# A two-model network on one core: expert numbers on GpSimd, rows restored by ScalarE, and 18 more gathered rows summed by TensorE

## The chip, the cores and the metric

The kernel runs on one core of a Trainium2 chip. The time is the device time of one execution in microseconds (us). Executions of the same kernel are compared by their median; lower is better. The core has five engines that work at the same time, each with its own queue of instructions: TensorE (PE, with its weight loads as PEld), VectorE (DVE), ScalarE (ACT), GpSimd (POOL) and SyncE (SP, which only issues DMAs). They meet at semaphores. Sixteen DMA engines move data between HBM and the core's memory.

## The reference, cut to what matters

Two networks of depth 2 run one after the other over 256 tokens of width 1024 in fp32. The change lies in the first one's expert layer (`_peer`) and in the work that is run beside it.

```python
def _peer(h, wq, sub_k1, sub_k2, u_tab, v_tab):
    q = (h @ wq).reshape(Bb, S, PEER_HEADS, 2, PEER_HALF)
    s1 = jnp.einsum('bshd,hnd->bshn', q[..., 0, :], sub_k1).astype(jnp.float32)
    s2 = jnp.einsum('bshd,hnd->bshn', q[..., 1, :], sub_k2).astype(jnp.float32)
    v1, i1 = lax.top_k(s1, PEER_TOPK)
    v2, i2 = lax.top_k(s2, PEER_TOPK)
    cand_s = (v1[..., :, None] + v2[..., None, :]).reshape(Bb, S, PEER_HEADS, PEER_TOPK * PEER_TOPK)
    cand_e = (i1[..., :, None] * PEER_N_KEYS + i2[..., None, :]).reshape(Bb, S, PEER_HEADS, PEER_TOPK * PEER_TOPK)
    top_s, pos = lax.top_k(cand_s, PEER_TOPK)
    experts = jnp.take_along_axis(cand_e, pos, axis=-1)
    g = jax.nn.softmax(top_s, axis=-1)
    ...
        u = jnp.take(u_tab, eb, axis=0)
        act = jax.nn.gelu(jnp.einsum('tkd,td->tk', u, hb), approximate=False)
        vv = jnp.take(v_tab, eb, axis=0)
        return jnp.einsum('tk,tkd->td', gb * act, vv)
```

Each token picks 8 heads x 16 = 128 experts. For each it needs a row of `u_tab` (a dot with the token's h) and a row of `v_tab` (added with its weight). The expert's number is i1 * 128 + i2 of the chosen pair. Around that stand attention, a short convolution, modulation by a condition (`ada`), and layer norms. The second network (`second_block`) has a pass over 256 context tokens, which does not depend on the first network, and a pass over the latent tokens, which follows it.

## The kernel before, in words

**Tiles and stages.** 256 tokens are two tiles t of 128 (one token on each partition). For each layer l and tile t there are two gather stages: `stage(l, t, 0, plan)` (dots with rows of `peer_u`) and `stage(l, t, 1, plan)` (sums of rows of `peer_v`). A stage has 32 rounds of 4 picks. For each pick GpSimd issues one indirect DMA (L1322), which fetches 128 rows of 4 KB, one for each token, into one of NS = 9 slots (six in RING, three at the end of WORK; the trace names them RING and WORK). VectorE makes the dot (`dots`, L2055) from the slot and the token's h, which lies in `hrows` (HB, two banks of PSUM), and writes the result to ACTS. In a sums stage (`sums`, L2073) it adds rows in turn to ACC and to HB. A slot is free for the gather nine later when it has been read. GpSimd has nothing else to do: its queue holds gathers in order, each behind a wait for its slot, the first of a group of 32 also behind `routed`.

**What is run beside them.** VectorE's order is written out by hand. `plan` maps a round to steps, which are Python generators: after round k's dots or sums the next piece of each named generator is issued. `c0` is the context pass of layer 0, `c1` the keys and values of the context for layer 1, `a` is `tile1(1, t)`, all of layer 1 for tile t up to its routing (with `closing` for the last norm of a tile), `choices` the routing groups of layer 0. Routing (`route`) treats 2 of 8 heads at a time: 4 groups a tile, 16 in all, 5 steps each: the top 16 of each half's 128 scores, the 256 sums of pairs, their top 16, and then the numbering (L2020 to L2030): with the place of the pick in the 16 x 16 table split into two places BF, VectorE compares each with iota, multiplies by the index TIF and adds up, once for each half. Of layer 0's groups one runs before the first dots stage and seven beside it, one or two steps a round; layer 1's groups run beside the two sums stages after.

**TensorE and SyncE.** TensorE works through a stream of weight chunks of 1 MB; SyncE loads them in the same order, three chunks ahead. TensorE's order is: layer 1's modulation, the context pass, `tile1(1, 0)`, `tile1(1, 1)`, the rest of the context pass, `c1`, then the latent pass. It also takes part in two sums stages: of the picks in `BY_PE`, 24 in stage (0, 1) and 36 in stage (1, 0), it multiplies the slot by a diagonal matrix of the weights (DIAG, made by ScalarE, L1623) into two banks (L882), and VectorE folds these into ACC (L2100).

**ScalarE** copies banks out of PSUM, in an order of its own. In the first dots stage it runs `ada("b1", [0], FIRST)` to its end before it comes to `gelu(0, 0)`, which closes the stage.

**The end of a sums stage** (VectorE): HB += ACC (L2102), HB *= gate (L2104), X = ALPHA * X + HB (L2106), moments of X (L2116 to L2124). At the start of the next dots stage the next tile's h is copied from HN to HB (L2081). `scaled_rows` (L2138, L2141) and `standard` (L2148, the y that TensorE waits for in `tile1`) are the first steps of `a`.

## Time and profile before

| | us |
|---|---|
| median of 3 runs | 2729.15 (2726.39 to 2731.91) |
| the profiled execution | 2727.62 |
| its span, first to last instruction | 2725.6 |
| first dots stage, layer 0 tile 0 | 216.0 to 496.4 |
| sums of layer 0 tile 0 | 496.4 to 725.2 |
| dots, sums of layer 0 tile 1 | 731.8 to 941.6, to 1161.0 |
| dots, sums of layer 1 tile 0 | 1168.7 to 1379.6, to 1585.0 |
| dots, sums of layer 1 tile 1 | 1592.5 to 1823.5, to 2025.1 |
| latent pass | 2025.1 to 2725.6 |

Busy time over the span: TensorE 1869.9 us (69%), VectorE 1862.3 us (68%), GpSimd 1074.6 us (39%), ScalarE 405.3 us (15%). DMA moves 850.48 MB, 538.17 MB of it gathers issued by GpSimd and 310.76 MB mostly weights issued by SyncE.

How to read the rows: a window row gives the busy time of each engine in a stretch, with the number of instructions, then TensorE's granted clock as a share of full speed, the busy share of the DMA engines (it can pass 1 a little) and what they moved. A timeline row gives start, duration, engine, source line, operation, what it writes and reads, shape, count, and in brackets the engine's idle time before it with what ended it. A group row gives busy time, the mean in ns of one, and idle time before.

### The profile page before, as it was taken

How to read it: one execution, taken by the hardware profiler on the slowest of the kernel's cores; microseconds unless marked ns; L12 is line 12 of the kernel's file. 1: busy time of each engine (PE TensorE's matmuls, PEld its weight loads, DVE VectorE, ACT ScalarE, POOL GpSimd, SP SyncE). 2: the span in 40 equal slices, each digit the busy share in tenths (PEclk: the TensorE clock that was granted, in tenths of full speed). 3: DMA queues.
4: the chain of work that ended last, by engine and by line, in shares of the span. 5: the costliest groups of instructions: out<-in, count | busy, mean ns of one | idle time of the engine just before them, and what ended most of it. 6: DMA issues, size and time to landing. Idle time of an engine off the chain costs nothing.

```text
span 2725.6 us, 24342 instructions
## 1 busy us (share of the span) xinstructions
PE 1869.9 (69%) x8469; PEld 1349.1 (49%) x8469; DVE 1862.3 (68%) x3405; ACT 405.3 (15%) x911; POOL 1074.6 (39%) x1059
## 2 busy tenths in 40 slices
PE   7988444385554373744635789774409999999998
PEld 5777111164443161233333277632307887578873
DVE  2758998879878879988888986778985342253001
ACT  1321001123103011012111010000104100141000
POOL 2004435567556555755565764556740000000000
PEclk9999556595776675967767999887659999999999
DMA  9629999999899999999999999999963694333443
GB/s 341 236 78 361 399 399 400 397 367 396 310 395 404 399 401 400 383 340 403 404 397 367 381 367 400 400 409 384 346 267 110 222 302 143 135 110 105 150 148 123
DMA packets 347386, 850.48 MB, mean 312 GB/s; under 512 B 23832, under 2 KB 126592, under 8 KB 347136
## 3 DMA queue, kind: packets, MB, share of 16 engines
q0 software_dynamic: 148672, 538.17, 51.1%
q1 hardware_dynamic: 198592, 310.76, 32.3%
q8 instruction: 68, 1.11, 0.2%
q14 instruction: 54, 0.44, 0.0%
HBM read 847.79 MB, written 1.05 MB: 311 GB/s over the span
## 4 chain that ended last, share of the span: by engine, by line
PE 29%; DMA 28%; DVE 21%; issue 14%; POOL 5%; ACT 1%; SPq 1%; DVEq 0%; POOLq 0%; ACTq 0%
DMA RING<-in_peer_u,EX 12%; DMA RING<-in_peer_v,EX 11%; PE bank L1174 10%; PE bank L1193 6%; POOL RING L1322 4%; DVE ACC L2055 3%; DMA WORK<-in_peer_u,EX 3%; PE bank L453 3%; DVE hrows L2073 2%; PE bank L1098 2%; POOL WORK L1322 2%; DMA WORK<-in_peer_v,EX 1%; PE bank L917 1%; PE bank L462 1%; PE bank L441 1%
## 5 line engine op out<-in xcount | busy, mean ns | idle before, releaser
L2055 DVE SCALAR_TENSOR_TENSOR ACC<-RING,hrows 128x1024 bf16<-128x1024 f32 x343 | 408.5, 1219 | 103.1 <-DMA RING<-in_peer_u,EX 96.2
L1322 POOL DMA_INDIRECT RING<-in_peer_u,EX x343 | 325.0, 948 | 350.2 <-DVE ACC L2055 244.1
L1322 POOL DMA_INDIRECT RING<-in_peer_v,EX x341 | 377.2, 1106 | 198.9 <-DVE hrows L2073 77.6
L1174 PE MATMUL bank<-HT,W 128*128 128x256 f32 x1280 | 276.6, 379 | 0.0
L1174 PEld LDWEIGHTS bank<-HT,W 128*128 128x128 f32 x1280 | 243.0, 190 | 33.0
L490 PE MATMUL bank<-W,CACT 128*32 128x512 f32 x544 | 115.2, 946 | 199.7 <-DMA W<-in_w_ada 115.4
L1193 PE MATMUL bank<-W,WORK 128*128 128x512 f32 x528 | 228.9, 596 | 18.6 <-DVE WORK L2763 16.2
L2055 DVE SCALAR_TENSOR_TENSOR ACC<-WORK,hrows 128x1024 bf16<-128x1024 f32 x169 | 202.1, 1218 | 47.5 <-DMA WORK<-in_peer_u,EX 46.5
L1322 POOL DMA_INDIRECT WORK<-in_peer_v,EX x171 | 194.3, 1137 | 99.1 <-DVE hrows L2073 41.7
L1322 POOL DMA_INDIRECT WORK<-in_peer_u,EX x169 | 160.9, 952 | 157.5 <-DVE ACC L2055 136.0
L2073 DVE SCALAR_TENSOR_TENSOR ACC<-RING,ACTS,ACC 128x1024 f32<-128x1024 f32 x148 | 189.9, 1283 | 35.3 <-DMA RING<-in_peer_v,EX 34.2
L2073 DVE SCALAR_TENSOR_TENSOR hrows<-RING,ACTS,hrows 128x1024 f32<-128x1024 f32 x147 | 189.1, 1286 | 29.9 <-DMA RING<-in_peer_v,EX 28.9
L441 PE MATMUL bank<-consts,XN 128*128 128x128 f32 x152 | 32.2, 387 | 239.5 <-DVE XN L2148 117.0
L1156 PE MATMUL bank<-HT,W 128*128 128x256 f32 x704 | 160.6, 390 | 20.7 <-DVE WORK L2763 14.0
L1193 PEld LDWEIGHTS bank<-W,WORK 128*128 128x128 f32 x528 | 100.7, 191 | 145.5 <-issue 142.4
L2769 DVE TENSOR_TENSOR WORK<-WORK,bank 128x256 f32<-128x256 f32 x44 | 18.5, 421 | 223.9 <-ACT WORK L1769 223.9
L1156 PEld LDWEIGHTS bank<-HT,W 128*128 128x128 f32 x704 | 136.6, 196 | 44.4 <-issue 22.0
L744 PE MATMUL bank<-HT,W 128*128 128x128 f32 x832 | 119.9, 313 | 51.6 <-DMA W<-in_peer_wq 27.8
L441 PEld LDWEIGHTS bank<-consts,XN 128*128 128x128 f32 x152 | 26.9, 204 | 242.0 <-DVE XN L2148 117.8
L490 PEld LDWEIGHTS bank<-W,CACT 128*32 128x32 f32 x544 | 14.7, 134 | 263.6 <-DMA W<-in_w_ada 99.7
L744 PEld LDWEIGHTS bank<-HT,W 128*128 128x128 f32 x832 | 117.0, 228 | 55.4 <-DMA W<-in_peer_wq 27.3
L1357 ACT ACTIVATE WORK<-bank 128x512 f32<-128x512 f32 (+5 forms) x167 | 87.4, 542 | 378.9 <-PE bank L744 124.5
(438 smaller groups left out, 3017.6 us busy)
## 6 DMA issues: line engine op xcount, KB each, us to landing
W<-in_ada_w SPq DMA_DIRECT2D x36, 1024.0 KB, 16.3
W<-in_w_gate SPq DMA_DIRECT2D x33, 1024.0 KB, 8.3
W<-in_w_up SPq DMA_DIRECT2D x33, 1024.0 KB, 5.5
W<-in_w_down SPq DMA_DIRECT2D x33, 1024.0 KB, 5.0
W<-in_w_in SPq DMA_DIRECT2D x32, 1024.0 KB, 16.4
W<-in_w_ada SPq DMA_DIRECT2D x32, 1024.0 KB, 16.9
W<-in_peer_wq SPq DMA_DIRECT2D x24, 1024.0 KB, 18.2
W<-in_w_o SPq DMA_DIRECT2D x10, 1024.0 KB, 15.9
```

Source lines behind the costliest of these rows:

```text
L441: mm = pe.transpose(b[0:rows, j * P:(j + 1) * P], a, ident)
L453: mm = pe.matmul(b[:, t * 256:t * 256 + cols], hT[:, k, t * P:(t + 1) * P], w[:, k, 0:cols], start=(k == 0), stop=(k == K - 1))
L490: mm = pe.matmul(b[32 * k:32 * k + 32, :], CACT[:, 4 * c + k, :], w[:, k, :], start=(c == 0), stop=(c == 1), skip_group_check=True)
L744: mm = pe.matmul(b[:, at:at + P], w[:, k, at:at + P], HT[:, 4 * c + k, T], start=first, stop=(c == 1 and k == 3), skip_group_check=True)
L1098: mm = pe.matmul(b[:, at_ * 256:(at_ + 1) * 256], HT[:, k, t * P:(t + 1) * P], w[:, k, :], start=(k == 0), stop=(k == DC - 1))
L1156: mm = pe.matmul(bs[u][:, e * S:(e + 1) * S], w[:, k, at_:at_ + P], HT[:, nk * part + k, :], start=(part == e == k == 0), stop=(part == n ...
L1174: mm = pe.matmul(bs[j][:, g * S:(g + 1) * S], w[:, k, j * P:(j + 1) * P], HT[:, k, :], start=(k == 0 and g == 0), stop=(k == DC - 1 and g ...
L1193: mm = pe.matmul(bs[2 * t + hf][:, :], GU[:, 2 * c + k, t * P:(t + 1) * P], w[:, k, hf * 512:(hf + 1) * 512], start=(c == 0 and k == 0), s ...
L1322: gp.indirect_dma_start(SLOT[g % NS], None, rows, bass.IndirectOffsetOnAxis(EX[:, t, k:k + 1], 0))\
L1357: free(name, A(out_, b[:, :] if src is None else src(b), ACT.Copy, scale=scale))
L2055: ve.scalar_tensor_tensor(out=JUNK[:, g % 2, :], in0=SLOT[g % NS], scalar=1.0, in1=HB[:, :], op0=ALU.mult, op1=ALU.mult, accum_out=ACTS[:, ...
L2073: ins = ve.scalar_tensor_tensor(out=acc, in0=SLOT[g % NS], scalar=ACTS[:, k:k + 1], in1=acc, op0=ALU.mult, op1=ALU.add)
```

## The change

It has three parts.

**Expert numbers.** Both halves' comparisons are done in one instruction over 1024 numbers into a larger EQ; the index of the first half is scaled by 128 and shifted by the layer's offset beforehand (TIF). For layer 0's seven groups beside the first dots stage VectorE stops after the comparison (`picked`), and GpSimd multiplies and adds in seven instructions, each behind the one before (`expert_numbers`), in its own queue between two gathers: `NUMBERED_AT` puts a group's numbering ahead of the gather that is nine behind the first pick of the second round after the comparison. VectorE waits for `routed` of the group before in the fourth step of each group, as TIF and EQ are used again. The other nine groups stay on VectorE in the wider form. ScalarE's `gelu(0, 0)` comes after three steps of `ada("b1", [0], FIRST)`, the rest after it.

**The seam.** At the end of a sums stage the total goes to ACC; ScalarE then copies HN to HB (`rows_again`), VectorE waits for that and writes the gated total to HN. Adding it to X and the moments are a step of their own (`into_rows`), the first of `a`, after round 0 of the next stage.

**The last sums stage.** TensorE also sums 18 picks of stage (1, 1), picks 36 to 70, every other one (`diagonal_rows(2)`), ahead of `c1` in its order. The result is folded in after round 19. The steps of `c1` and the first latent rows come later (22 instead of 14, 24 instead of 18), and some steps of `c0` in the stage before one or two rounds sooner.

Semaphores that can be shared are merged, and a few steps of the context pass are moved by one or two rounds. The diff, cut to its core:

```diff
-        BY_PE = {(0, 1): [78 + 2 * i for i in range(24)], (1, 0): [54 + 2 * i for i in range(36)]}
+        SHARED = [(0, 1), (1, 0), (1, 1)]
+        BY_PE = {(0, 1): [78 + 2 * i for i in range(24)], (1, 0): [54 + 2 * i for i in range(36)],
+                 (1, 1): [36 + 2 * i for i in range(18)]}
...
+        ROUTE_STEPS = 5
+        FIRST_STEPS = [1 + k % 2 for k in range(PICKS // 4)]
+        LATER_ROUNDS = [8 + (23 * i) // 20 for i in range(ROUTE_STEPS * GROUPS)]
+        def round_of_first(step):
+            return next(k for k in range(len(FIRST_STEPS)) if sum(FIRST_STEPS[:k + 1]) > step)
+        NUMBERED_AT = {}
+        for i_, (t_, g_) in enumerate([(0, g) for g in range(1, GROUPS)] + [(1, g) for g in range(GROUPS)]):
+            NUMBERED_AT[gather(0, 0, 0, 4 * (round_of_first(ROUTE_STEPS * i_ + 3) + 2)) + NS] = (0, t_, g_)
+        def groups_routed(l, t, g):
+            return (l * NT + t) * GROUPS + g
+        def expert_numbers(eng, do, settle, l, t, g):
+            do(eng.tensor_tensor(EQ, EQ, TIF.unsqueeze(2).to_broadcast([P, GSETS, TOPK, TOPK]), ALU.mult))
+            settle()
+            eq = EQ.rearrange("p (h e) k a -> p h e k a", e=2)
+            part = eq[:, :, 0, :, :]
+            do(eng.tensor_tensor(part, part, eq[:, :, 1, :, :], ALU.add))
+            width = TOPK
+            while width > 1:
+                width //= 2
+                settle()
+                do(eng.tensor_tensor(part[:, :, :, 0:width], part[:, :, :, 0:width], part[:, :, :, width:2 * width], ALU.add))
+            settle()
+            do(eng.tensor_copy(EX[:, t, g * GP:(g + 1) * GP].rearrange("p (h k) -> p h k", h=GHEADS), part[:, :, :, 0]),
+               mark("routed", "all"))
         def place(n):
...
+            def diagonal_rows(u):
+                ls, ts = SHARED[u]
+                picks = BY_PE[ls, ts]
+                bs = [open_bank(("sum", ("b1", u), hf), "V") for hf in range(2)]
+                pe.wait_ge(mark("diag", "b1"), u + 1)
+                for i, k in enumerate(picks):
+                    g = gather(ls, ts, 1, k)
+                    pe.wait_ge(rows_in[g % NS], 16 * (g // NS + 1))
+                    for hf in range(2):
+                        mm = pe.matmul(bs[hf][:, :], DIAG[u][:, i, :], SLOT[g % NS][:, hf * 512:(hf + 1) * 512],
+                                       start=(i == 0), stop=(i == len(picks) - 1))
+                        if hf == 0 and i == len(picks) - 1:
+                            mm.then_inc(filled, 1)
+                    mm.then_inc(slots_passed, 1)
+                pe.matmul(bs[1][0:1, 0:1], ident[0:1, 0:1], ident[0:1, 1:2], start=False, stop=True, skip_group_check=True).then_inc(filled, 1)
...
             last_rows.append(nrows[0])
+            diagonal_rows(2)
...
+                            if g in NUMBERED_AT:
+                                lg, tg, group = NUMBERED_AT[g]
+                                gp.wait_ge(mark("picked", "all"), groups_routed(lg, tg, group))
+                                expert_numbers(gp, do, settle, lg, tg, group)
                             if table == 0 and k % GP == 0:
-                                gp.wait_ge(mark("routed", f"b{l}"), t * GROUPS + k // GP + 1)
+                                gp.wait_ge(mark("routed", "all"), groups_routed(l, t, k // GP) + 1)
                             if g >= NS:
...
+            def rows_again(i):
+                act.wait_ge(mark("totalled", "all"), i)
+                do(A(HB[:, :], HN[:, :], ACT.Copy), mark("restored", "all"))
...
             weigh(0, 0)
-            all_of(ada("b1", [0], FIRST))
+            first = ada("b1", [0], FIRST)
+            for _ in range(3):
+                next(first)
             gelu(0, 0)
+            all_of(first)
             spread_rows()
...
             next(c0)
+            rows_again(1)
             root1("b0", 0, 7)
...
                 if t:
+                    rows_again(2)
                     root1("b0", t, 7 + t)
...
             spread_rows()
+            rows_again(3)
...
-                bp = BP.rearrange("p h k -> p (h k)")
-                do(ve.tensor_scalar(BQ[:, 0, :], bp, 4, None, ALU.logical_shift_right))
-                do(ve.tensor_scalar(BQ[:, 1, :], bp, TOPK - 1, None, ALU.bitwise_and))
-                settle()
-                do(ve.tensor_copy(BF, BQ))
+                n = groups_routed(l, t, g)
+                if n:
+                    ve.wait_ge(mark("routed", "all"), n)
+                tif = TIF.rearrange("p (h e) k -> p h e k", e=2)
+                ti = TI.rearrange("p (h e) k -> p h e k", e=2)
+                do(ve.tensor_scalar(tif[:, :, 0, :], ti[:, :, 0, :], float(KEYS), float(l * EXPERTS), ALU.mult, ALU.add))
+                do(ve.tensor_copy(tif[:, :, 1, :], ti[:, :, 1, :]))
+                do(ve.tensor_scalar(BQ[:, :, 0, :], BP, 4, None, ALU.logical_shift_right))
+                do(ve.tensor_scalar(BQ[:, :, 1, :], BP, TOPK - 1, None, ALU.bitwise_and))
+                settle()
+                do(ve.tensor_copy(BF.rearrange("p (h e) k -> p h e k", e=2), BQ))
                 do(ve.tensor_tensor(GW[:, t, picks].rearrange("p (h k) -> p h k", h=GHEADS), BV,
                                     BV[:, :, 0:1].to_broadcast([P, GHEADS, TOPK]), ALU.subtract),
                    v_step if g < GROUPS - 1 else mark("tx", p))
                 settle()
+                where = [P, GSETS, TOPK, TOPK]
+                by_gpsimd = 0 < n < NT * GROUPS
+                do(ve.tensor_tensor(EQ, BF.unsqueeze(3).to_broadcast(where),
+                                    const("iota").unsqueeze(1).unsqueeze(1).to_broadcast(where), ALU.is_equal),
+                   mark("picked", "all") if by_gpsimd else v_step)
                 yield
-                tif = TIF.rearrange("p (h e) k -> p h e k", e=2)
-                eq = EQ.rearrange("p (h k a) -> p h k a", h=GHEADS, k=TOPK)
-                eqn = EQ.rearrange("p (n a) -> p n a", a=TOPK)
-                for e in range(2):
-                    do(ve.tensor_tensor(eqn, BF[:, e, :].unsqueeze(2).to_broadcast([P, GP, TOPK]),
-                                        const("iota").unsqueeze(1).to_broadcast([P, GP, TOPK]), ALU.is_equal))
-                    settle()
-                    do(ve.tensor_tensor(eq, eq, tif[:, :, e, :].unsqueeze(2).to_broadcast(full), ALU.mult))
-                    settle()
-                    do(ve.tensor_reduce(EF[:, e, :], eqn, AX.X, ALU.add))
-                    settle()
-                do(ve.scalar_tensor_tensor(out=EF[:, 0, :], in0=EF[:, 0, :], scalar=float(KEYS), in1=EF[:, 1, :],
-                                           op0=ALU.mult, op1=ALU.add))
-                settle()
-                do(ve.tensor_scalar(EX[:, t, picks], EF[:, 0, :], float(l * EXPERTS), None, ALU.add), mark("routed", p))
+                if not by_gpsimd:
+                    settle()
+                    do(ve.tensor_tensor(EQ, EQ, TIF.unsqueeze(2).to_broadcast(where), ALU.mult))
+                    settle()
+                    do(ve.tensor_reduce(EF, EQ, AX.X, ALU.add))
+                    settle()
+                    ef = EF.rearrange("p (h e) k -> p h e k", e=2)
+                    do(ve.tensor_tensor(EX[:, t, picks].rearrange("p (h k) -> p h k", h=GHEADS), ef[:, :, 0, :], ef[:, :, 1, :], ALU.add),
+                       mark("routed", "all"))
                 yield
...
+            def fold(u):
+                for hf in range(2):
+                    b = wait_full(ve, ("sum", ("b1", u), hf))
+                    c = slice(hf * 512, (hf + 1) * 512)
+                    free(("sum", ("b1", u), hf), ve.tensor_tensor(ACC[:, c], ACC[:, c], b[:, :], ALU.add))
+                settle()
+            def last_fold(k):
+                ve.wait_ge(slots_free, vector_done(gather(1, 1, 1, PER * (k + 1))))
+                fold(2)
+                yield
             def stage(l, t, table, plan):
                 p = f"b{l}"
-                if table == 0 and (l or t):
-                    do(ve.tensor_copy(HB[:, :], HN[:, :]))
-                    settle()
...
-                if (l, t) in SHARED:
-                    q = ("b1", SHARED.index((l, t)))
-                    for hf in range(2):
-                        b = wait_full(ve, ("sum", q, hf))
-                        c = slice(hf * 512, (hf + 1) * 512)
-                        free(("sum", q, hf), ve.tensor_tensor(ACC[:, c], ACC[:, c], b[:, :], ALU.add))
-                    settle()
-                do(ve.tensor_tensor(HB[:, :], HB[:, :], ACC[:, :], ALU.add))
-                settle()
-                do(ve.tensor_tensor(HB[:, :], HB[:, :], GA[:, GATES[p, 0][1], :], ALU.mult))
-                settle()
-                do(ve.scalar_tensor_tensor(out=X[:, t, :], in0=X[:, t, :], scalar=ALPHA, in1=HB[:, :],
+                if (l, t) in SHARED[:2]:
+                    fold(SHARED.index((l, t)))
+                last = l == LAYERS - 1 and t == NT - 1
+                do(ve.tensor_tensor(ACC[:, :], HB[:, :], ACC[:, :], ALU.add), v_step if last else mark("totalled", "all"))
+                settle()
+                if not last:
+                    ve.wait_ge(mark("restored", "all"), n[mark("totalled", "all").name])
+                do(ve.tensor_tensor(HN[:, :], ACC[:, :], GA[:, GATES[p, 0][1], :], ALU.mult))
+                settle()
+            def into_rows(l, t):
+                p = f"b{l}"
+                do(ve.scalar_tensor_tensor(out=X[:, t, :], in0=X[:, t, :], scalar=ALPHA, in1=HN[:, :],
                                            op0=ALU.mult, op1=ALU.add))
                 settle()
                 moments(p, t)
...
+                into_rows(l - 1, t)
+                yield
                 scaled_rows(f"b{l - 1}", t)
...
+                if p == "c0":
+                    ve.wait_ge(mark("routed", "all"), groups_routed(1, 0, 0))
                 if who == "c":
...
-                    if not kv_only:
+                    if kv_only:
+                        yield
+                    else:
                         yield from gate_rows(p, (1, 2))
...
             def closing(l, t):
+                into_rows(l, t)
+                yield
                 scaled_rows(f"b{l}", t)
                 yield
...
-            stage(0, 0, 1, {k: [c0] for k in (0, 3, 5, 10, 16, 20, 21, 25, 31)})
+            stage(0, 0, 1, {k: [c0] for k in (0, 5, 6, 11, 16, 20, 21, 25, 31)})
             for t in range(NT):
                 a = tile1(1, t)
-                stage(t, 1 - t, 0, {k: [a] for k in (0, 1, 4, 11, 12, 14, 16, 17, 19, 23, 28)})
-                plan = {**{k: [a] for k in (0, 1)}, **{8 + (23 * i) // 20: [a] for i in range(5 * GROUPS)}}
+                stage(t, 1 - t, 0, {k: [a] for k in (0, 1, 2, 4, 11, 12, 14, 16, 17, 19, 23, 28)})
+                plan = {k: [a] for k in (0, 1, *LATER_ROUNDS)}
                 if t:
                     plan[15] = plan.get(15, []) + [c0]
                 stage(t, 1 - t, 1, plan)
                 finish(a)
             a = closing(1, 0)
-            stage(1, 1, 0, {0: [a], **{k: [c0] for k in (4, 5, 9, 10, 13, 14, 18, 19, 22, 23, 26)}})
-            stage(1, 1, 1, {6: [c0], 8: [c0], 10: [c1], 14: [c1], 18: [first_rows()]})
+            stage(1, 1, 0, {**{k: [a] for k in (0, 1)}, **{k: [c0] for k in (4, 5, 9, 10, 13, 14, 17, 18, 21, 22, 24)}})
+            stage(1, 1, 1, {6: [c0], 8: [c0], 10: [c1], 11: [c1], 19: [last_fold(19)], 22: [c1], 24: [first_rows()]})
             finish(c0, c1, closing(1, 1))
             for p, l in (("l0", 0), ("l1", 1)):
```

## Rows read from the trace of the kernel before

**Rows 1.** Page, 40 slices of the span: busy tenths of the DMA engines

```profile
DMA  9629999999899999999999999999963694333443
```

**Rows 2.** Windows: the gather half, then D00, S00, S01, D11 and S11

```profile
216.00:2025.10 1809.10, 1012.79 (x4295) 684.70 (x4293) 1543.83 (x2738) 234.65 (x522) 1053.86 (x1021) 0.74 1.00 386
216.00:496.40 280.40, 151.67 (x665) 79.30 (x664) 255.12 (x697) 31.15 (x60) 125.37 (x134) 0.62 1.03 396
496.40:725.20 228.80, 140.90 (x650) 112.36 (x648) 192.66 (x201) 46.56 (x116) 153.22 (x128) 0.72 1.01 384
...
941.60:1161.00 219.40, 120.55 (x538) 74.39 (x538) 193.46 (x364) 26.03 (x63) 138.08 (x125) 0.74 1.02 395
...
1592.50:1823.50 231.00, 194.05 (x780) 151.38 (x779) 165.94 (x275) 11.73 (x18) 120.36 (x128) 0.92 1.02 397
1823.50:2025.10 201.60, 76.31 (x246) 46.76 (x244) 175.37 (x165) 15.82 (x33) 134.65 (x119) 0.69 0.96 370
```

**Rows 3.** DMA queues from 1625 to 1700 us: packets, MB, share of 16 engines

```profile
q0 software_dynamic: 5328, 19.40, 66.0%
q1 hardware_dynamic: 5327, 10.58, 37.1%
```

**Rows 4.** Timeline of VectorE in S11, two sums back to back

```profile
1885.79 1.28 DVE L2073 SCALAR_TENSOR_TENSOR ACC<-RING,ACTS,ACC 128x1024 f32<-128x1024 f32 x1
1886.99 1.28 DVE L2073 SCALAR_TENSOR_TENSOR hrows<-RING,ACTS,hrows 128x1024 f32<-128x1024 f32 x1
```

**Rows 5.** Timeline of VectorE from S00's last sum to the second dot of D01

```profile
725.16 1.23 DVE L2102 TENSOR_TENSOR hrows<-hrows,ACC 128x1024 f32<-128x1024 f32 x1
...
730.58 1.22 DVE L2081 COPY hrows<-HN 128x1024 f32<-128x1024 f32 x1
731.84 1.22 DVE L2055 SCALAR_TENSOR_TENSOR ACC<-RING,hrows 128x1024 bf16<-128x1024 f32 x1
...
732.98 1.22 DVE L2055 SCALAR_TENSOR_TENSOR ACC<-RING,hrows 128x1024 bf16<-128x1024 f32 x1
```

**Rows 6.** Timeline of GpSimd in S11, two gather issues

```profile
1964.37 0.93 POOL L1322 DMA_INDIRECT RING<-in_peer_v,EX  x1 [0.30 <-issue]
1965.61 1.99 POOL L1322 DMA_INDIRECT RING<-in_peer_v,EX  x1 [0.31 <-DVE hrows L2073]
```

**Rows 7.** Timeline of VectorE, first and last of the eight of a group's numbering

```profile
206.53 0.69 DVE L2020 TENSOR_TENSOR WORK<-WORK,consts 128x512 f32<-128x512 f32 x1
...
211.10 0.18 DVE L2030 TENSOR_SCALAR EX<-WORK 128x32 uint32<-128x32 f32 x1
```

**Rows 8.** Window: D00 while groups are routed

```profile
216.00:440.20 224.20, 127.55 (x557) 67.27 (x559) 215.54 (x628) 24.29 (x47) 95.39 (x102) 0.64 1.03 395
```

**Rows 9.** Windows: a stretch of S00, and S00's last sum to D01's y

```profile
550.00:575.00 25.00, 23.45 (x109) 20.06 (x108) 21.11 (x18) 3.77 (x8) 19.82 (x18) 0.99 0.93 336
714.90:747.70 32.80, 4.47 (x37) 4.18 (x35) 29.95 (x51) 7.31 (x12) 8.50 (x9) 0.60 0.66 241
```

**Rows 10.** Timeline of ScalarE: the third step's copy, and the table load of gelu

```profile
461.84 0.17 ACT L1357 ACTIVATE CR<-bank 128x4 f32<-128x4 f32 x1 [1.17 <-PE bank L499]
...
493.29 1.28 ACT L1638 ACT_TABLE_LOAD   x1
```

**Rows 11.** Window: S10 with routing beside it

```profile
1465.00:1530.00 65.00, 36.17 (x69) 13.15 (x70) 62.67 (x151) 5.36 (x19) 43.67 (x40) 0.84 0.94 351
```

**Rows 12.** Timeline of ScalarE: one pass over 128x1024

```profile
2033.72 1.06 ACT L1375 ACTIVATE XN<-X 128x1024 f32<-128x1024 f32 x1 [2.88 <-DVE X L2141]
```

**Rows 13.** S11 from round 8 on: the window, and GpSimd's larger group there

```profile
1884.60:2025.10 140.50, 29.00 (x112) 24.03 (x112) 132.15 (x125) 10.00 (x23) 99.16 (x89) 0.59 0.94 356
...
L1322 POOL DMA_INDIRECT RING<-in_peer_v,EX x60 | 67.1, 1119 | 25.9 <-issue 15.5 <-DVE hrows L2073 10.3
```

**Rows 14.** Timeline of TensorE in S10, its first rows and a later one

```profile
1479.97 8.30 PE L882 MATMUL bank<-RING,WORK 128*128 128x512 f32 x12 [20.95 <-DMA RING<-in_peer_v,EX]
...
1491.57 1.98 PE L882 MATMUL bank<-RING,WORK 128*128 128x512 f32 x4 [1.59 <-DMA RING<-in_peer_v,EX]
```

86 lines of the change are left out of this document (37 added, 49 removed).

## The prediction, made before the changed kernel was run

> **What bounds the kernel now.** I read the page first: the DMA engines are busy 90% or more in nearly all slices from the fourth to the twenty-ninth (204 to 1976 us), and a third to a half near the end [rows 1]. So there are two halves. Up to 2025 us rows of the expert tables are gathered; from there on TensorE is busy nearly all the time, and nothing in the change touches that. Then I cut the first half at the eight gather stages. I call them D00, S00, D01, S01, D10, S10, D11, S11 (D dots, S sums; layer, tile). Each gathers 128 times a row of 4 KB for 128 tokens, 0.524 MB. In all eight the DMA share is 0.96 to 1.03, at 370 to 397 GB/s; the rows show five of them, the lowest and the highest among them [rows 2]. The forecast rests on that: VectorE is busy 72 to 91% of the stages, but beside a queue that is as full.
>
> How full is full? In a stretch of D11 in which VectorE mostly waits, the gathers get 19.40 MB in 75 us (259 GB/s, a row in 2.03 us) and the weights 10.58 MB (141 GB/s), 400 GB/s together [rows 3]. Without weights a row costs 0.524/0.400 = 1.31 us. VectorE needs 1.19 us for a sum issued back to back and 1.14 us for a dot, GpSimd 0.94 us for an issue and 0.30 us between two [rows 4 to 6]. These rates lie close together, so time freed on VectorE is worth only what DMA then moves more. The first half moves 386 GB/s over 1809 us, 698 MB [rows 2]; at 400 GB/s that is 1745 us. The 64 us between are the most that could be found here, and they are spread thin.
>
> **Part 1, expert numbers.** Sixteen routing groups. The numbering of one is eight VectorE instructions from 206.53 to 211.28 us, 4.75 us [rows 7]. The new form handles all 1024 numbers at once. An instruction over 128x1024 takes 1.22 to 1.23 us and 0.04 to the next [rows 5], so compare, multiply and reduce cost 3 x 1.26, the last add 0.2, one more small scaling 0.1: 4.1 us, a gain of 0.65 us for each of nine groups. Of the seven groups routed beside D00, VectorE keeps the compare and the scaling, 1.36 us instead of 4.75: 3.4 us each, 23.8 us together. Until 440 us VectorE is busy 215.5 of 224.2 us there, so it paces the dots [rows 8]. With 23.8 us less D00 would last 256.6 us; but beside unbounded weights 128 rows need 128 x 2.03 = 260 us. D00 becomes about 20 us shorter.
>
> That is not 20 us of the kernel. D00's DMA share is 1.03 with 111 MB [rows 2]. If it ends 20 us sooner, 8 MB of weights have not come, and S00 wants them, for layer 1's modulation and for the context block. D00 and S00 together move 199 MB in 509.2 us; at 400 GB/s it is 497.5, so at most 11.7 us can be had. What keeps S00 below that (336 GB/s while TensorE is busy 23.5 of 25 us with the context block's projections [rows 9]) isn't touched. I take 5 us, bounds 0 and 12.
>
> What GpSimd's seven arithmetic instructions for a group cost, no row shows. The nearest rows are its own issues: 7 x (0.94 + 0.30) = 8.7 us [rows 6]. From below, VectorE's 1.23 us for 1024 elements [rows 5], scaled to the 2048 of all seven, is 2.5 us; from above, an issue of 1.99 us gives 7 x 2.3 = 16 us [rows 6]. I take 8.7 us. Queued behind it are the gathers: with nine slots up to 9 x 2.03 = 18 us of rows are on their way, so 8.7 us without an issue starves nothing. VectorE waits for it only in the fourth step of the next group; between lie at least eight dots (9.1 us) and three steps of some 3 us, about 18 us. The page GPSIMD Engine Reference of the Trainium skill (section 3.1) speaks against the move: a two-input elementwise pass takes 2.6 cycles an element at 1.2 GHz there, about twice VectorE's time. By it the 2048 elements are an estimated 4.5 us and what seven starts cost; no row of this kernel shows that.
>
> On ScalarE, `gelu` is moved ahead of the second half of layer 1's first modulation. Now ScalarE reaches it at 493.3 us, 1.8 us before the dots end; the three steps that then stand ahead of it end at 462 us [rows 10]. Without that, it would be late by what D00 gains. Its price: two banks stay uncopied until D00 ends, and the rows for the context block's second step (round 5, no longer 3) come later. A wait there leaves the bandwidth to the weights; I cost it at nothing, and it is why the 12 us are not reached. If that cover is gone, it is the 5 us.
>
> The layer 1 groups lie beside S01 and S10, 4 x 0.65 = 2.6 us each, partly in stretches where VectorE is busy 63 of 65 us and DMA moves 351 GB/s [rows 11]: 1.5 us in S01 (395 GB/s) and 2.5 us in S10, bounds 0 and 5 for both.
>
> **Part 2, the seam from sums to the next dots (three times).** Now 725.16 to 731.84 us, 6.7 us [rows 5]. Afterwards: the add (1.26), then a copy into hrows by ScalarE that VectorE waits for (nearest row 1.06 us over 128x1024 [rows 12], with the hand-over 1.3), then the multiply (1.26), 3.8 us. The rest, 2.9 us, is done after four dots. VectorE drops its own copy of 1.22 us and gains a wait of 1.3, so its line is not shorter. Slots come free 2.9 us sooner, but TensorE gets the tile's y after twelve dots instead of eight, 4.6 us later. The window from the last sums to y moves 241 GB/s [rows 9], so there is room; yet what is gained ahead of the moved step is given back in it. I take 0 for D01 and D10 and 1 us for D11, where TensorE awaits no y. Bounds: 3 x 2.9 = 8.7 us gained, 3 us lost.
>
> **Part 3, S11.** From round 8 (1884.6 us) to the end 96 rows and a few weights, 356 GB/s x 140.5 us = 50 MB, pass with VectorE busy 132.2 us [rows 13]. TensorE takes 18 rows, 18 x 1.19 = 21.4 us, and the fold adds 2 x 0.69 (the nearest row is 128x512 [rows 7]): VectorE 112 us. DMA needs 50/0.400 = 125 us. So the bound passes to DMA, or to GpSimd, whose issue takes 1.12 us here [rows 13] and 0.30 between: 1.42 us a row, 136 us if it stayed so slow. I take 129.5 us, a gain of 11, bounds 5 and 15. TensorE's price for a row is 1.98 us, one every 2.62 us; the first three after idleness take 8.3 us, in which slots are held [rows 14]. The diagonals are made by ScalarE behind `gelu`, long before round 9. The context keys (round 22, not 14) and the latent rows (24, not 18) come later; TensorE has 28 rows x 1.31 = 37 us for what follows, some 20 us of transposes and projections, so nothing sticks out past the last sum. If it did, it would cost up to 13 us. The context block's steps in D11 that come one or two rounds sooner move no bytes. The chain after S11 (add, multiply, residual, norm) has the same length.
>
> **Sum.** 5 + 1.5 + 2.5 + 1 + 11 = 21 us. The profiled run took 2727.6 us for a span of 2725.6, 1.5 us under the median of 2729.15; from the median it gives **2708 us**.
>
> **Rivals.**
> 1. D00's gain carries through, 20 us and not 5: the deferred weights find room. 2729 - 36 = 2693 us. For it: S00 moves 384 GB/s. Against: D00's share of 1.03 [rows 2].
> 2. Gathers are bound by GpSimd's issue once VectorE is eased, D00 gives nothing, S11 6 us and the routing 4: 2719 us. For it: 1.42 us a row in S11 [rows 13].
> 3. Slower: the numbering takes GpSimd T a group. In the 3.3 rounds of a group it must also issue 13.3 rows, 13.3 x 1.24 = 16.5 us. From T = 18 us on, seven periods of 16.5 + T use up the 16 us that the other parts bring; at T = 20 us the routed part of D00 is 7 x 36.5 = 255 us, not 224, and the kernel takes 2729 + 31 - 16 = 2744 us. The place is the fourth step of each group, where VectorE would wait on `routed`. Against: 20 us is above the bound of 16.
> 4. TensorE's rows ease little, as S11 waits for DMA already: 3 us there, 10 elsewhere, 2716 us. Against: 356 GB/s [rows 13].
>
> The page DMA: Bandwidth & Descriptors of the Trainium skill (section Queues, rings and completion order) says that a DMA engine takes turns between its rings packet by packet. The trace agrees in that the split stays near 259 to 141 GB/s. By that rule weights put off by D00 come at a fixed share beside the gathers, which speaks against rival 1.
>
> **Chances.** Forecast 0.58, rival 1 0.12, rival 2 0.12, rival 4 0.10, rival 3 0.08. About 0.2% (5.5 us) is what a measurement of this kernel can tell from no change. Faster by more, under 2723.7 us, are the forecast and rivals 1, 2 and 4 less their tails: 0.84; within 0.2%, those tails and mild cases of rival 3: 0.10; slower 0.06. The range goes from 2691 us (rival 1) to 2723 us (rival 2 with S11 near its lower bound); rival 3 is left out.
>
> **What would show it.** D00 at 256 to 264 us with the DMA share still near 1.0, and S00 longer by 10 to 18 us; GpSimd's arithmetic at 6 to 12 us a group; seams of 3.8 us, with D01 and D10 as long as before, the 2.9 us inside; S11 at 188 to 192 us, VectorE idle for rows, over 385 GB/s after round 8; from the last sum on 700 us as now. It would be wrong if VectorE waited for GpSimd in D00, if S00 stayed at 229 us, or if DMA stayed under 360 GB/s in S11 after round 8.

## The result and the profile after

The changed kernel takes 2711.4 us, the median of 4 runs (2706.26 to 2713.43), beside 2727.77 us for the kernel before on the same chip: a ratio of 0.995, with a 95% interval from 0.9936 to 0.9964. That is 14 us less by the ratio, 16 by the medians; 21 were forecast. Measured again on another chip it came to 2710.67 beside 2723.41 us, 0.9959 (0.9943 to 0.9975), 11 to 13 us. The profiled execution took 2706.26 us for a span of 2704.3, the fastest of its four.

Windows of the changed kernel, in the columns of [rows 2]: the gather half, then D00, S00, S01, S10 with its seam, D11, S11 and the part of S11 from round 8 on.

```profile
212.30:2006.80 1794.50, 1044.89 (x4371) 694.21 (x4369) 1491.94 (x2653) 243.39 (x544) 1084.78 (x1070) 0.75 1.01 389
212.30:485.40 273.10, 134.20 (x595) 68.62 (x593) 233.54 (x654) 29.71 (x56) 164.20 (x183) 0.64 1.03 397
485.40:721.60 236.20, 154.77 (x720) 120.42 (x720) 194.70 (x203) 49.67 (x122) 150.03 (x128) 0.74 1.02 388
933.50:1156.40 222.90, 119.93 (x546) 73.36 (x546) 194.71 (x356) 27.37 (x65) 140.10 (x129) 0.75 1.02 397
1369.70:1581.40 211.70, 132.70 (x529) 83.08 (x530) 183.82 (x352) 32.00 (x78) 140.84 (x130) 0.83 1.01 384
1581.40:1817.00 235.60, 205.77 (x801) 156.50 (x800) 168.49 (x280) 11.13 (x17) 120.92 (x128) 0.93 1.02 396
1817.00:2006.80 189.80, 98.96 (x286) 53.16 (x284) 155.12 (x149) 21.26 (x51) 128.44 (x119) 0.78 1.00 381
1874.70:2006.80 132.10, 66.63 (x186) 37.05 (x186) 111.68 (x109) 10.08 (x23) 98.69 (x89) 0.76 0.98 373
```

VectorE works 22 us less in D00 and 20 us less in S11 than in [rows 2], and the whole half is only some 15 us shorter: the DMA share was 1.00 already and is 1.01 now. The table gives each stage from its first row to the next stage's first row, so a seam counts with the stage ahead of it. "First" is the first dot, "tail" what follows the last sum. The kernels under the second line are those of the experiments, one profiled execution each.

| us | first | D00 | S00 | D01 | S01 | D10 | S10 | D11 | S11 | tail |
|---|---|---|---|---|---|---|---|---|---|---|
| before | 216.0 | 280.4 | 235.5 | 209.8 | 227.1 | 210.9 | 212.9 | 231.0 | 201.6 | 700.5 |
| changed | 212.3 | 273.1 | 236.2 | 211.9 | 222.9 | 213.4 | 211.7 | 235.6 | 189.8 | 697.4 |
| changed, again | 215.1 | 271.7 | 238.8 | 211.4 | 223.1 | 213.2 | 208.5 | 235.6 | 189.1 | 701.2 |
| third part undone | 214.1 | 271.2 | 242.3 | 211.9 | 222.7 | 213.5 | 211.9 | 235.3 | 196.7 | 698.2 |
| numbers on VectorE | 213.2 | 278.9 | 235.5 | 212.4 | 222.6 | 213.0 | 208.4 | 235.4 | 190.8 | 701.7 |
| gelu behind one step | 211.8 | 266.9 | 244.8 | 212.1 | 222.6 | 212.8 | 213.0 | 236.0 | 191.4 | 701.8 |
| restore first | 216.0 | 269.6 | 241.7 | 211.9 | 222.8 | 213.1 | 206.2 | 236.8 | 188.5 | 701.8 |
| old seam | 213.8 | 270.4 | 240.4 | 208.8 | 225.6 | 211.1 | 208.9 | 235.5 | 188.2 | 697.6 |
| 26 rows | 213.6 | 270.9 | 240.1 | 211.8 | 222.8 | 213.7 | 212.0 | 236.3 | 190.5 | 701.2 |
| slow numbers | 213.5 | 295.7 | 228.3 | 211.5 | 222.6 | 213.4 | 210.3 | 235.4 | 188.9 | 700.7 |
| sums in PSUM | 214.2 | 272.2 | 239.1 | 211.5 | 223.0 | 212.8 | 208.8 | 236.7 | 190.3 | 701.4 |
| third part alone | 215.7 | 290.6 | 233.1 | 209.8 | 225.7 | 211.6 | 206.5 | 235.0 | 190.5 | 700.6 |
| half rows | 215.8 | 241.7 | 233.5 | 212.4 | 222.6 | 213.1 | 213.0 | 236.5 | 187.8 | 701.3 |
| three together | 213.5 | 269.6 | 237.7 | 212.2 | 222.6 | 213.6 | 207.3 | 236.6 | 189.7 | 700.6 |

Where the code of a stage is the same, the first dot lies between 211.8 and 216.0 us, S10 between 208.4 and 213.0 and the tail between 697.4 and 701.8: these scatter by 4 to 5 us from one execution to the next. So do the first two stages: D00 and S00 together take 507.4 to 513.5 us in the seven traces of kernels that leave them as changed, and of the kernel before there is one trace, with 515.8. D01, S01, D10 and D11 repeat within 2 us. The changed kernel's profiled execution had luck at both ends (most of 3.7 us, and 3.1), which is why its span is 21 us under that of before and its median only 16.

Two things in it were not foreseen. First, the end of D00: VectorE's last dot, its wait for gelu, and the first sum; then ScalarE, with what it waited for.

```profile
476.40 1.22 DVE L2118 SCALAR_TENSOR_TENSOR ACC<-RING,hrows 128x1024 bf16<-128x1024 f32 x1 [0.81 <-DMA RING<-in_peer_u,EX]
...
485.11 0.29 DVE L2166 TENSOR_TENSOR ACTS<-ACTS,GW 128x128 f32<-128x128 f32 x1 [6.54 <-ACT ACTS L1690]
485.44 1.29 DVE L2134 TENSOR_SCALAR hrows<-RING,ACTS 128x1024 f32<-128x1024 f32 x1
```

```profile
481.44 0.60 ACT L1400 ACTIVATE ROWT<-bank 128x512 f32<-128x512 f32 x1 [14.37 <-PE bank L522]
483.21 0.17 ACT L1400 ACTIVATE CR<-bank 128x4 f32<-128x4 f32 x1 [1.17 <-PE bank L531]
483.40 1.28 ACT L1690 ACT_TABLE_LOAD   x1
```

The three steps that stand ahead of gelu ended at 462 us before [rows 10] and at 483.4 us now. They hang on TensorE, and TensorE on weights, which come later: up to 462 us SyncE's queue has moved 35.4 MB since D00 began, where it had moved 38.4 before, and the gathers 63.4 MB instead of 58.8. Second, the third seam:

```profile
1571.92 1.23 DVE L2172 TENSOR_TENSOR ACC<-hrows,ACC 128x1024 f32<-128x1024 f32 x1
1580.14 1.23 DVE L2176 TENSOR_TENSOR HN<-ACC,GA 128x1024 f32<-128x1024 f32 x1 [7.00 <-ACT hrows L1678]
1581.40 1.22 DVE L2118 SCALAR_TENSOR_TENSOR ACC<-RING,hrows 128x1024 bf16<-128x1024 f32 x1
```

```profile
1578.53 0.60 ACT L1400 ACTIVATE ROWS<-bank 128x512 f32<-128x512 f32 x1 [0.32 <-PE bank L466]
1579.02 1.02 ACT L1678 ACTIVATE hrows<-HN 128x1024 f32<-128x1024 f32 x1
```

VectorE waits 1.2 us for the restore at the first seam, 1.5 at the second and 7.0 at the third, where ScalarE's order puts four copies of norm rows ahead of it, and TensorE makes those only once it has finished its 36 rows of S10.

### The profile page after: what moved, and what is told of

It is laid out like the page before. It is cut to its first block, busy times and chain, and to the rows that moved or that the text cites. A ratio compares the mean times of both kernels' runs of the same rounds, so it can differ in the third digit from the quotient of the medians.

```text
span 2704.3 us, 24477 instructions
## 1 busy us (share of the span) xinstructions
PE 1895.4 (70%) x8543; PEld 1353.6 (50%) x8543; DVE 1809.6 (67%) x3317; ACT 413.6 (15%) x932; POOL 1105.8 (41%) x1108
## 3 DMA queue, kind: packets, MB, share of 16 engines
q8 instruction: 68, 1.11, 0.2%
## 4 chain that ended last, share of the span: by engine, by line
PE 34%; DMA 31%; DVE 15%; issue 11%; POOL 5%; ACT 2%; SPq 1%; DVEq 0%; POOLq 0%; ACTq 0%
DMA RING<-in_peer_u,EX 11%; PE bank L1210 10%; DMA RING<-in_peer_v,EX 9%; PE bank L1229 6%; DMA W<-in_ada_w 3%; POOL RING L1379 3%; PE bank L485 3%; DVE ACC L2118 3%; DMA WORK<-in_peer_u,EX 2%; DMA WORK<-in_peer_v,EX 2%; PE bank L494 2%; PE bank L1134 2%; POOL WORK L1379 2%; DVE hrows L2136 2%; PE bank L473 2%
## 5 line engine op out<-in xcount | busy, mean ns | idle before, releaser
L1379 POOL DMA_INDIRECT RING<-in_peer_v,EX x341 | 371.0, 1088 | 197.8 <-issue 72.3
L2136 DVE SCALAR_TENSOR_TENSOR ACC<-RING,ACTS,ACC 128x1024 f32<-128x1024 f32 x142 | 182.1, 1282 | 39.7 <-DMA RING<-in_peer_v,EX 39.1
L2136 DVE SCALAR_TENSOR_TENSOR hrows<-RING,ACTS,hrows 128x1024 f32<-128x1024 f32 x141 | 181.4, 1286 | 34.5 <-DMA RING<-in_peer_v,EX 33.8
L791 PE MATMUL bank<-RING,WORK 128*128 128x512 f32 x212 | 110.0, 647 | 95.8 <-DMA RING<-in_peer_v,EX 95.8
```

The lines of the kernel that those rows point to most:

```text
L791: mm = pe.matmul(bs[hf][:, :], DIAG[u][:, i, :], SLOT[g % NS][:, hf * 512:(hf + 1) * 512], start=(i == 0), stop=(i == len(picks) - 1))
L1379: gp.indirect_dma_start(SLOT[g % NS], None, rows, bass.IndirectOffsetOnAxis(EX[:, t, k:k + 1], 0))\
L2136: ins = ve.scalar_tensor_tensor(out=acc, in0=SLOT[g % NS], scalar=ACTS[:, k:k + 1], in1=acc, op0=ALU.mult, op1=ALU.add)
```

## The experiments

"Ratio" is always the kernel's time to that of the kernel before on the same chip, with the 95% interval. 0.001 is 2.7 us.

**The changed kernel again.** No edit.

> The changed kernel once more, so that single parts can be compared with it. 2711 us, within 3. Theory: the 6.5 us for which VectorE waits for gelu at the end of the first dots stage and the 7.0 us for which it waits for ScalarE's restore at the third seam come again, since both stand behind work of TensorE in ScalarE's order. The 3.7 us by which the first dot came earlier (212.3 instead of 216.0 us) and the 3.1 us of the latent pass are 0.65 us and 0 by the change and otherwise scatter: first dot near 214, latent pass near 700. Rival: they are the change's, and both come again to 0.5 us.

Measured: 2710.67 us, ratio 0.9959 (0.9943 to 0.9975). First dot at 215.1, tail 701.2: both were scatter. The two waits come again, somewhat shorter, 4.74 and 5.98 us.

**The third part undone.**

```diff
-        SHARED = [(0, 1), (1, 0), (1, 1)]
+        SHARED = [(0, 1), (1, 0)]
...
-            diagonal_rows(2)
...
-            diagonals(2)
...
-            stage(1, 1, 1, {6: [c0], 8: [c0], 10: [c1], 11: [c1], 19: [last_fold(19)], 22: [c1], 24: [first_rows()]})
+            stage(1, 1, 1, {6: [c0], 8: [c0], 10: [c1, c1], 14: [c1], 18: [first_rows()]})
```

> The third part undone: VectorE sums all 128 rows of the last sums stage, no diagonals for it, its steps in rounds 6, 8, 10, 14 and 18 as before; the first two parts stay. Theory (what TensorE takes is worth 11 us): the stage goes back to 201 us from 189.8, the kernel to 2722 us. Rival: part of the 11.8 us that the stage lost are weights that the dots stage before has taken (28.7 MB instead of 26.3 there, 6.9 instead of 9.3 in the sums): 2.4 MB are 6 us, then the stage takes only 196 us and the kernel 2717. Rival 4 of the prediction: 2714 us.

Measured: 2720.38 us, ratio 0.9993 (0.9979 to 1.0006), so 9 to 10 us more than the changed kernel, while S11 takes 196.7 us, as the rival said. Both hold in part: the time is the theory's, the stage the rival's. In the profiled executions the rest of the distance lies in S00 and S10, the stages that scatter; that it is nothing but scatter isn't shown. Without a single row on TensorE S11 is already 4.9 us shorter than in the kernel before. D11 has taken 2.3 MB of its weights and is 4.3 us longer, which fits, though no run tried the weights by themselves. The hardware queue in D11, before and with the third part undone:

```profile
q1 hardware_dynamic: 12727, 26.38, 29.9%
```

```profile
q1 hardware_dynamic: 13315, 28.65, 31.9%
```

So the third part itself is worth 7 us in the two last stages (432.0 us together here, 424.7 in the repeated run), nearly all of what lies between those and the 432.6 us of the kernel before.

**Numbers on VectorE**, in the wide form.

```diff
-            NUMBERED_AT[gather(0, 0, 0, 4 * (round_of_first(ROUTE_STEPS * i_ + 3) + 2)) + NS] = (0, t_, g_)
+            pass
...
-                by_gpsimd = 0 < n < NT * GROUPS
+                by_gpsimd = False
```

> The numbering of layer 0's seven groups stays on VectorE, in the wider form (4.1 us a group); all else as changed. VectorE has 7 x 2.7 = 19 us more in the first dots stage. Theory (the stage is bound by DMA after the change, and the first two stages share 198 MB): the dots take 278 us instead of 265, the wait of 6.5 us for gelu goes, and the first two stages together take 512 to 515 us instead of 509.3: 2714 to 2717 us. Rival A: VectorE's time carries through, 19 us less the wait of 6.5: 2724 us. Rival B: GpSimd's numbering brings nothing: 2711 us.

Measured: 2714.55 us, ratio 0.9969 (0.9959 to 0.998): 3 to 4 us more, with intervals that overlap. The dots of D00 take 277.6 us instead of 265.7, and the wait for gelu is gone, as the theory has it. 17 us more of VectorE's time in D00 cost 7.2 us there and 3.9 after S00 (514.4 us together instead of 510.5), little beyond the scatter of these two stages. Rival A, 2724 us, is excluded; that the numbering on GpSimd brings the kernel something (against rival B) is likely and not clear of noise.

**Gelu behind one step.**

```diff
-            for _ in range(3):
+            for _ in range(1):
                 next(first)
             gelu(0, 0)
```

> ScalarE issues gelu behind one step of layer 1's first modulation instead of three. Now the third step ends at 483.4 us, 5.1 us after VectorE has weights ready, since TensorE waits for weights until 479.4. The table load then lies beside the dots, and VectorE's wait of 6.5 us shrinks to under 0.5 us. Theory (the queue stays full in the wait: 400 GB/s from 475 to 490 us, so the weights have used it): the first sums stage gets back 4 to 6 of the 6.5 us, the kernel gains 0 to 2 us: 2710 us. Rival: the wait is on the path, all of it is gained: 2705 us.

Measured: 2712.68 us, ratio 0.996 (0.9948 to 0.9972), no gain. D00 and S00 of this kernel:

```profile
211.80:478.70 266.90, 131.31 (x588) 67.44 (x586) 233.47 (x655) 29.22 (x54) 164.43 (x183) 0.65 1.03 396
478.70:723.50 244.80, 159.76 (x736) 124.22 (x728) 195.44 (x203) 50.48 (x124) 146.22 (x128) 0.72 1.02 385
```

The wait is gone and D00 is 5 us shorter, S00 is 6 us longer, and the two take 511.7 us beside 510.5. So this wait of VectorE, during which DMA moved 399 GB/s (changed kernel, 475 to 490 us), cost nothing that could be measured.

**Restore ahead of the norm rows.**

```diff
-            spread_rows()
             rows_again(3)
+            spread_rows()
             root1("b1", 0, 9)
```

> At the third seam ScalarE restores h (its copy of HN into HB) before the four copies of norm rows, not behind them. Now VectorE waits 7.0 us there (the rows wait for TensorE, which makes them until 1578.5 us), at the other two seams 1.2 and 1.5 us. The wait shrinks to about 1.5 us. Theory (no weights are under way there, and the gathers move 155 to 219 GB/s from 1581 to 1591 us, so the queue is not full): the 5.5 us are gained, the seam takes 5 us instead of 10, and the dots stage after it stays at 234 us: the kernel 2705 to 2707 us beside 2711. Rival: the dots stage after it is bound by DMA and by TensorE's weights, which don't come sooner: no gain, 2711 us, and the dots stage gets 4 to 5 us longer, as at the other seams.

Measured: 2708.82 us, ratio 0.9942 (0.9926 to 0.9958). VectorE's wait falls to 1.16 us:

```profile
1577.62 1.22 DVE L2172 TENSOR_TENSOR ACC<-hrows,ACC 128x1024 f32<-128x1024 f32 x1
1580.01 1.23 DVE L2176 TENSOR_TENSOR HN<-ACC,GA 128x1024 f32<-128x1024 f32 x1 [1.16 <-ACT hrows L1678]
```

From the last sum to the next dot, with the fold, it is 5.0 us, not 10.8 and 9.8 as in the two runs of the changed kernel. D11 takes 1.2 us more, so 3.6 us should be left. The two kernels run beside it on the same chip, which both have the time of the changed one within the interval, took 2709.74 and 2709.93 us. What is left of the gain is 1 us by these medians and can't be told from none.

**The old seam**, with the rest as changed.

```diff
-                do(ve.tensor_tensor(ACC[:, :], HB[:, :], ACC[:, :], ALU.add), v_step if last else mark("totalled", "all"))
+                do(ve.tensor_tensor(HB[:, :], HB[:, :], ACC[:, :], ALU.add))
...
+                if table == 0 and (l or t):
+                    do(ve.tensor_copy(HB[:, :], HN[:, :]))
...
```

> The second part undone: at all three seams VectorE adds into HB, multiplies, adds to X, takes the moments and copies HN to HB itself before the next dots, 6.7 us; ScalarE's restore is gone, and so is the wait for it. The rest as changed. Theory of the prediction (0 + 0 + 1 us for the three seams): 2711 to 2713 us beside 2711; the first two seams get 2.5 to 2.9 us longer and the dots stages after them 2 to 2.5 us shorter; at the third the wait of 7.0 us goes, the seam takes 8 us instead of 9.8 to 11, and the kernel may even gain 1 to 2 us. Rival: the seam is worth its 2.9 us three times, 2718 us.

Measured: 2709.74 us, ratio 0.9948 (0.9933 to 0.9963). S01 with its seam is 2.5 us longer and D10 behind it 2.1 us shorter; D01 is 2.6 us shorter. The new seam is worth nothing that can be measured: at the first two the stage behind gives the gain back, and at the third the wait makes it longer than the old one (9.8 and 10.8 us with the fold, beside 8.0).

**26 rows instead of 18.**

```diff
-                 (1, 1): [36 + 2 * i for i in range(18)]}
+                 (1, 1): [36 + 2 * i for i in range(26)]}
...
-            stage(1, 1, 1, {..., 19: [last_fold(19)], 22: [c1], 24: [first_rows()]})
+            stage(1, 1, 1, {..., 23: [last_fold(23)], 25: [c1], 26: [first_rows()]})
```

> TensorE sums 26 rows of the last sums stage instead of 18 (picks 36 to 86, every other one); folded in after round 23 instead of 19, the next step of c1 in round 25 instead of 22, first latent rows 26 instead of 24. VectorE has 8 x 1.19 = 9.5 us less in the stage. Theory (18 rows have already handed the stage to DMA and to GpSimd's issue; 381 GB/s): the stage loses at most 2 us of 189.5, and what follows the fold lies closer to the end: 2709 to 2713 us. Rival: VectorE's time is still the bound; 18 rows brought 7.6 us, 0.42 us a row, so 8 rows bring 3.4 us: 2707 us.

Measured: 2709.93 us, ratio 0.9945 (0.9931 to 0.996); S11 190.5 us. VectorE is busy 145.5 instead of 155.1 us in it, and the stage is no shorter: 18 rows have used the effect up.

**Slow numbers.**

```diff
         def expert_numbers(eng, do, settle, l, t, g):
+            for _ in range(5):
+                do(eng.tensor_tensor(EQ, EQ, EQ, ALU.mult))
+                settle()
```

> GpSimd does five more passes over 128x1024 (EQ times EQ, which leaves its zeros and ones) ahead of each of the seven numberings: 6.04 + 5 x 2.4 = 18 us a group. It asks for the price in rival 3 of the prediction. Theory: a group's 13.3 rows take 27.6 us at the present pace, and GpSimd needs 16.5 + 18 = 34.6 us, so it becomes the bound: the first dots stage gets 7 x 7 = 49 us longer (320 us), weights come early in it, the first sums stage gets 20 to 28 us shorter (VectorE is busy 203 of its 238 us): the kernel 2731 to 2741 us. Rival: what 9 slots hold (18 us of rows) covers it and VectorE's wait on routed stays under 2 us a group: under 2715 us.

Measured: 2726.45 us, ratio 1.0014 (1.0003 to 1.0024), 16 us more than the changed kernel. The numbering of the changed kernel, then the five added passes and the last instruction of the slow one:

```profile
248.88 2.37 POOL L331 TENSOR_TENSOR WORK<-WORK 128x1024 f32<-128x1024 f32 x1
251.33 1.27 POOL L335 TENSOR_TENSOR WORK<-WORK 128x512 f32<-128x512 f32 x1
252.68 1.95 POOL L340 TENSOR_TENSOR WORK<-WORK 128x256 f32<-128x256 f32 x4
254.69 0.23 POOL L342 CAST EX<-WORK 128x32 uint32<-128x32 f32 x1
```

```profile
251.34 9.79 POOL L332 TENSOR_TENSOR WORK<-WORK 128x1024 f32<-128x1024 f32 x5
...
267.34 0.23 POOL L345 CAST EX<-WORK 128x32 uint32<-128x32 f32 x1
```

The numbering takes 6.0 us a group in the changed kernel and 16.2 us here. D00 is 24 us longer than in the repeated run, S00 10.4 shorter. VectorE never waits for `routed`; it waits for rows, 51 us instead of 32 in D00, that GpSimd issued late. GpSimd is busy 233 of D00's 296 us. Hence ten more microseconds a group take away all that the change has brought.

**Sums of S11 in PSUM only.**

```diff
-                    acc = ACC[:, :] if n % 2 else HB[:, :]
-                    ve.wait_ge(slots_free, n - 1)
+                    alone = (l, t) == (1, 1)
+                    acc = ACC[:, :] if n % 2 and not alone else HB[:, :]
+                    ve.wait_ge(slots_free, n if alone else n - 1)
...
```

> In the last sums stage VectorE adds every row to HB (in PSUM) and none to ACC (in SBUF); the fold copies TensorE's sum into ACC. Each sum then waits for the one before: 1.31 us apart instead of 1.19, 110 x 0.12 = 13 us more for VectorE. What is asked: why the stage's end moves only 374 to 384 GB/s. In the changed kernel GpSimd's issues that begin under a sum into HB take 0.936 us (34 of 34), those that begin under a sum into ACC, which reads two operands from SBUF, 1.35 us in the mean, three in four of them longer than 1 us. From 1870 to 2007 us GpSimd is in an issue or between two for 126 of 137 us. Theory (the stage's end is bound by GpSimd's issues, and they are held up by the sums into ACC): all issues of the stage take 0.94 us, 91 rows need 91 x 1.31 = 119 us by DMA instead of 126, the stage takes 181 to 185 us instead of 189, the kernel 2703 to 2707 us. Rival A: DMA is the bound anyway and the issues don't matter: 189 us, 2710. Rival B: VectorE's 13 us more decide: 195 us or more, 2716.

Measured: 2713.96 us, ratio 0.9961 (0.9948 to 0.9973); S11 190.3 us. GpSimd's issues into RING from round 8 on (busy time, mean ns, idle before), of the changed kernel and of this one:

```profile
L1379 POOL DMA_INDIRECT RING<-in_peer_v,EX x60 | 66.2, 1104 | 18.4 <-issue 16.5 <-DVE hrows L2136 1.5 <-PE bank L791 0.4
```

```profile
L1379 POOL DMA_INDIRECT RING<-in_peer_v,EX x60 | 57.3, 956 | 23.3 <-DVE hrows L2137 14.4 <-issue 7.6 <-PE bank L791 1.3
```

And a window of each after 1900 us, in which no weights come:

```profile
1901.00:1949.00 48.00, 29.25 (x81) 14.43 (x82) 35.16 (x30) 3.86 (x8) 37.20 (x36) 0.86 1.00 381
```

```profile
1904.00:1950.00 46.00, 28.55 (x83) 14.63 (x82) 34.34 (x28) 3.86 (x8) 34.57 (x37) 0.85 1.03 409
```

The first half of the theory is shown: the issues take 0.956 us instead of 1.104, and DMA goes from 381 to 409 GB/s. In that stretch of the changed kernel 36 issues and the 0.30 us between two fill the 48 us, so GpSimd was the bound there. The second half is not: the last row lands 183.5 us after the stage's start instead of 187.3 and 188.2, but VectorE, whose sums are now 1.39 us apart, needs another 6.8 us instead of 1.7. What the issues gave back, the slower sums took, so neither rival is right by itself: the bound went from GpSimd to VectorE.

**The third part alone** (numbers on VectorE, old seam, gelu last).

```diff
             first = ada("b1", [0], FIRST)
-            for _ in range(3):
-                next(first)
-            gelu(0, 0)
             all_of(first)
+            gelu(0, 0)
...
```

> The third part alone: as the kernel with the old seam, and in addition layer 0's numbering stays on VectorE (in the wider form, the one thing left of the first part) and gelu stands behind the whole first modulation again. Theory: the kernel without the third part was 9.7 us over the changed one, numbers on VectorE cost 3.9 us, the old seam nothing, so the third part is most of the change: 2713 to 2715 us beside 2710 for the changed kernel and 2722 for the kernel before. Rival: the parts hold each other up (the weights that the first part puts off meet the last stages), and the third alone brings less than 5 us: 2718 us.

Measured: 2719.21 us, ratio 0.9983 (0.9973 to 0.9993), 4 to 5 us under the kernel before: the rival's number, by another cause. D11 and S11 take 425.5 us, so the third part brings its 7 us here too. But VectorE waits 11.8 us for gelu at the end of D00:

```profile
504.05 1.28 ACT L1690 ACT_TABLE_LOAD   x1
```

The dots end at 493.0 us, 2 us sooner than before, and ScalarE comes to gelu 11 us later than before [rows 10], behind steps that wait for weights. D00 and S00 together take 523.7 us, beside 515.8 in the kernel before. The run with numbers on VectorE has the same numbering and 514.4 us. Of the 9.3 us between them, 3.0 are the old seam, which D01 gives back (209.8 us instead of 212.4); the rest goes with the place of gelu. So the new place is likely what lets the first part pay; the old place with the numbering on GpSimd was not tried.

**Half rows in D00.**

```diff
+                            if NS <= g < PICKS:
+                                halves = d["peer_u"].rearrange("l e (h n) -> (l e h) n", h=2)
+                                gp.indirect_dma_start(SLOT[g % NS][:, 0:D // 2], None, halves, ...)
...
```

> The gathers of the first dots stage, but for the first nine, fetch 2 KB a token instead of 4 (the first half of a slot is filled, from another row, so the dots are of other data): 31 MB less. All instructions are the same in number and size on the other engines. What is asked: what bounds the first dots stage after the change. Theory (DMA): VectorE is busy 268 of the stage's 272 us with its last wait, but that counts what overlaps; of the dots' 265 us it waits 31 us for rows. The stage falls to VectorE's own work, 230 to 238 us, and the first sums stage, with the weights loaded earlier, to 215 to 225 us: the kernel 50 to 65 us shorter. Rival (VectorE and GpSimd pace the stage, and rows come when they come): less than 15 us shorter in the first dots stage.

Measured: 2675.68 us, ratio 0.9824 (0.9805 to 0.9842). Its D00:

```profile
215.80:457.50 241.70, 135.64 (x637) 69.41 (x636) 232.19 (x654) 30.66 (x59) 160.71 (x179) 0.67 0.94 332
```

With 31 MB less D00 is 30 us shorter and S00 5 us, 35 together, under the 50 to 65 that I expected, since VectorE and GpSimd follow closely. But the rival, under 15 us, is excluded: D00 of the changed kernel is held by DMA in the main.

**Three edits together.** The edits of sums in PSUM, 26 rows and restore first.

> Three edits together on the changed kernel: VectorE's sums of the last stage all go to HB in PSUM, TensorE takes 26 of its rows instead of 18 (with the later rounds of the run with 26 rows), and ScalarE restores h ahead of the norm rows at the third seam. Theory (at the stage's end three limits lie together: VectorE's time, GpSimd's issue of 1.39 us a row beside sums into ACC, and DMA's 1.28 to 1.31 us a row; each edit alone met the next one): sums into HB are 1.39 us apart and 102 of them 142 us, issues take 0.94 us, the gathers get over 400 GB/s without a break after 1900 us, the stage takes 182 to 185 us instead of 189.5, the third seam 5.0 instead of 9.8, and the kernel is 5 to 8 us under the changed one: a ratio to the kernel before of 0.992 to 0.994. Rival A: the stage is held by what VectorE does for the context block from 1875 to 1905 us and by the last rows alone: 188 to 190 us as in each run alone, ratio 0.994 to 0.996. Rival B: the weights are the bound of the last two stages together, and their sum stays at 424 to 427 us.

Measured: 2707.45 us, ratio 0.9944 (0.9932 to 0.9957). The third seam takes 5.0 us and DMA 410 GB/s from 1899 to 1947 us, yet S11 is 189.7 us long, as rival A has it. Its last row lands after 184.8 us, VectorE ends 4.9 us later: the last 41 rows are all VectorE's. No kernel here that does the whole work beats the changed one by more than the interval.

## Why the prediction was right, and where it was too high

The forecast was 2708 us and 21 us of gain. The measured gain is 11 to 16 us, inside the range of 2691 to 2723 us. The total alone doesn't decide for the forecast: from its own start of 2729.15 us the two ratios give 2715.5 and 2718.0 us, as near to rival 4 (2716) and rival 2 (2719). The stages do. Rival 4 gave the last stage 3 us, and the third part brought 7. Rival 2 gave D00 nothing, with gathers held by GpSimd's issue; half rows shorten D00 by 30 us at the same number of issues. At the end of S11 rival 2's mechanism is at work, as the sums in PSUM show. Step by step:

**D00 and S00 (5 us): right in its sum, with wrong pieces in it.** Together they went from 515.8 to 509.3 and 510.5 us, 5 to 6.5 less, the first seam's 3 among them, and to 510.6 in the mean of the seven traces that leave them as changed. D00 was to take 256 to 264 us and took 272 to 273: its dots took 265.3, and the wait for gelu the rest. That wait was costed by an event of the trace before, steps that end at 462 us, though these steps wait for weights and the same paragraph put the weights off. That it cost nothing was right, and for the reason given: the queue is full. S00, without its seam, was to be 10 to 18 us longer than 229 and took 232.5 and 235.1, 4 to 6 longer: both shifts were smaller than forecast, and their difference came out near 5. That is luck in part. Rival 1 (all of D00's gain carries through) is refuted: whatever D00 loses, S00 takes back in good part, most plainly with gelu behind one step. The split of 259 to 141 GB/s in [rows 3] has a plain reading that the prediction doesn't give: in those 75 us the two queues sent 5328 and 5327 packets, one for one, and the bytes split as the mean sizes of their packets, 3.6 and 2.0 KB.

**GpSimd's numbering (8.7 us, bounds 2.5 and 16): 6.0 measured.** The multiply over 128x1024 takes 2.37 us, where VectorE's takes 1.23. The page GPSIMD Engine Reference of the Trainium skill (section 3.1) gives about that ratio, 1.96; the trace agrees with 1.93. Its 4.5 us for 2048 elements in one pass stands beside 6.0 measured for seven instructions. It was right that what GpSimd doesn't issue in that time is covered: VectorE waited 32 us for rows in D00, and 51 only with slow numbers. Rival 3 set the point at which the change's gain is used up to 18 us a group, at VectorE's wait on `routed`. The run with slow numbers has it a little under 16.2 us, and in the gathers, not in that wait.

**S01 (1.5) and S10 (2.5).** Without its seam S01 took 220.4 us before and 218.6 to 219.1 after, as forecast, and D01 and S01 together gained 2.1 to 2.4 us. S10 without its seam took 206.2 us before and 199.8 to 204.6 in the thirteen runs after, so it did get shorter, by 1.6 to 6.4 us; no run undoes the wider form, so its share isn't shown. But D10 and S10 together took 423.8 us before and 421.5 to 426.2 in the runs that leave them and the third seam as changed: no clear gain. With the restore first or the old seam they took 418.1 to 420.9. The step that failed is the third seam.

**The seams (1 us).** The first two took 3.7 and 4.0 us instead of 6.7, where 3.8 were forecast. That they give back what they gain was right within 1.5 us: D01 and D10 are 1.6 to 2.8 us longer. The sign named for it, D01 and D10 as long as before, contradicts the 0 that the sum takes for them, and didn't come. The third seam was costed at 3.8 us like the others and took 9.5 and 8.5. I had the restore's duration from a row, but not what stands ahead of it in ScalarE's queue, which is in the code.

**S11 (11 us): right in its number, wrong in its ground.** It lost 11.7 to 12.5 us, of which the third part is 6.9 to 7.6 (196.7 to 189.8 and 189.1); 4.9 came without it, with 2.3 MB of weights that D11 took over, and D11 was 4.3 to 4.6 us longer. The sentence that failed, as far as the runs show it, is that the context block's steps in D11 "move no bytes". The weights moved in every run with the new rounds (28.5 to 29.1 MB in D11, not 26.4), also without the third part and with the old seam; that the rounds are the cause was not tried by itself. The term itself, put at 11, was 7: DMA was to come to 400 GB/s after round 8 and came to 373 and 377. What holds it there is the alternative that the prediction named and gave too little weight, GpSimd's issue: 89 rows in 132 us are 1.48 us a row, of which 1.11 are the issue and 0.30 the time between two. The 11.7 near the forecast's 11 is luck.

**The sum.** 5.9 (D00 and S00) + 2.2 (D01 and S01) + 0 (D10 and S10) + 7.5 (D11 and S11) is 15.6 us, beside 16 by the first medians and 13 by the second. None of the three signs of being wrong came: VectorE never waited for GpSimd's numbers in D00, S00 didn't stay at 229 us, and DMA stayed above 360 GB/s. Against the forecast's 21, 4.5 are missing in D11 and S11 (12 were forecast, with the third seam's 1) and 2.5 in D10 and S10 with the seam, and the first four stages gave 1.6 more.

## What to carry to other kernels

Where the DMA queue is full in every stage, as here, an engine's saved time is worth what the stages' bytes leave: add up neighbouring stages before you book a gain, since weights that one puts off or takes early are paid for in the other. When an edit makes one engine faster, look in the queues of those that it will meet for what stands ahead of the meeting, and ask what that in turn waits for; a time read from the old trace doesn't stay where it was. And where three limits lie within some per cent, as VectorE, GpSimd's issues and DMA in S11, easing one or even two of them shows in the engine's rows and not in the time.

## What the runs showed of the hardware

GpSimd's issue of an indirect DMA depends on what VectorE does beside it. In the four sums stages of the changed kernel, 140 issues began under a sum into HB, which reads the row in SBUF and the sum in PSUM: 139 took 0.93 to 0.94 us. One, begun in the sum's last 3%, took 1.97; VectorE's next instruction, which reads WORK in SBUF twice, had just begun. 176 began under a sum into ACC, which reads both in SBUF: 130 took over 1.0 us, up to 1.99, and the mean is 1.33 to 1.44 by stage. Those that began 6 to 93% of the way into such a sum ended 0.81 us after the sum did, however early they began (132 of 133). One of each kind, and the sums beside them:

```profile
1885.91 1.73 POOL L1379 DMA_INDIRECT WORK<-in_peer_v,EX  x1 [0.78 <-DVE hrows L2136]
1887.94 0.93 POOL L1379 DMA_INDIRECT WORK<-in_peer_v,EX  x1 [0.30 <-issue]
```

```profile
1885.54 1.28 DVE L2136 SCALAR_TENSOR_TENSOR ACC<-WORK,ACTS,ACC 128x1024 f32<-128x1024 f32 x1
1886.74 1.28 DVE L2136 SCALAR_TENSOR_TENSOR hrows<-RING,ACTS,hrows 128x1024 f32<-128x1024 f32 x1
1888.04 1.28 DVE L2136 SCALAR_TENSOR_TENSOR ACC<-RING,ACTS,ACC 128x1024 f32<-128x1024 f32 x1
```

The issue at 1885.91 us begins under a sum into ACC and ends 0.8 us after that sum; the one at 1887.94 us begins in the last tenth of a sum into HB and takes 0.93. With the sums of S11 in HB alone, none of the 76 issues of that stage that begin under a sum takes over 0.94 us. The Trainium skill, page SBUF — State Buffer, section SBUF: two separate sides, says that a VectorE instruction with two inputs from SBUF and a GpSimd instruction that reads SBUF shut each other out for the length of an instruction. By that rule an issue that finds a sum into ACC under way waits for its end; the trace agrees, also for a DMA's issue. The wait cost S11 28 GB/s after 1900 us (381 to 409). VectorE's sums in PSUM alone are 1.39 us apart instead of 1.19, so no time was won back here.
